# Another order for the tiles of the wide value group, and the convolution step ahead of the scans on DVE

## The reference

```python
hn = rmsnorm(x, norm_g)
z = jnp.einsum('bsd,de->bse', hn, w_in)
(aq, ak, av, ag, mq, mk, mv, mo, mi, mf, mg, gq, gk, gv, ga, gg) = jnp.split(z, split_idx, axis=-1)
att = band_chunk_attention(aq, ak, av, rel_bias)
y_a = att * jax.nn.silu(ag)
qk = jax.nn.silu(causal_conv(jnp.concatenate([mq, mk], axis=-1), conv_w))     # 4 taps
h_ml = mlstm_chunkwise(mq_c, mk_c, mv, mi + b_gates[:6], mf + b_gates[6:])
y_b = jax.nn.sigmoid(mo) * head_rmsnorm(h_ml, ml_norm_g, 6) * jax.nn.silu(mg)
log_alpha = jax.nn.log_sigmoid(jnp.einsum('bsr,rk->bsk', ga, w_alpha) + b_alpha) / 16
...
return x + jnp.einsum('bse,ed->bsd', jnp.concatenate([y_a, y_b, y_c], axis=-1), w_out)
```

## Time and profile before

| | |
|---|---|
| median of 3 runs | 1580.49 us (1580.3 to 1581.3) |
| the profiled execution | 1579.18 us, span 1577.5 us |
| instructions | 22092 |
| PE busy | 1531.3 us (97% of the span) |
| DVE, ACT, POOL busy | 826.8, 721.6, 318.2 us (52%, 46%, 20%) |
| mean granted TensorE clock | 0.992 of full speed |
| DMA | 127.99 MB, 81 GB/s on average |

### The profile page before, as it was taken

How to read it: one execution, slowest core, us unless ns; L and a number is a source line. 1 busy time by engine, 2 the same in 40 slices (tenths; PEclk the granted TensorE clock), 3 DMA queues, 4 the chain that set the end, 5 groups by cost and what they waited for, 6 DMA issues and landing times. The chain is left out here.

```text
span 1577.5 us, 22092 instructions
## 1 busy us (share of the span) xinstructions
PE 1531.3 (97%) x8990; PEld 1293.9 (82%) x8990; DVE 826.8 (52%) x1412; ACT 721.6 (46%) x1404; POOL 318.2 (20%) x273
## 2 busy tenths in 40 slices
PE   7998999999999999999999999999999999999999
PEld 6777888899889887788888888768887888888887
DVE  5326556657435754755334544568956644244442
ACT  4325554556664644544224443467854534133431
POOL 1000133101340001244103431032001343014420
PEclk9989999999999999999999999999999999999999
DMA  7212112223231102233323232110013323223331
GB/s 243 68 54 67 54 54 68 90 101 111 78 95 41 41 1 94 81 107 114 100 75 99 93 119 82 50 44 14 15 54 93 94 96 122 90 80 94 110 112 45
DMA packets 37518, 127.99 MB, mean 81 GB/s; under 512 B 4248, under 2 KB 8872, under 8 KB 37416
## 3 DMA queue, kind: packets, MB, share of 16 engines
q1 hardware_dynamic: 37416, 126.57, 25.1%
HBM read 124.46 MB, written 2.10 MB: 80 GB/s over the span
## 5 line engine op out<-in xcount | busy, mean ns | idle before, releaser
L321 PE MATMUL bank<-hhi,whi 128*128 128x512 f32 x1056 | 415.7, 394 | 4.5 <-ACT hhi L1970 1.8
L323 PE MATMUL bank<-hhi,wlo 128*128 128x512 f32 x1056 | 412.0, 390 | 0.0
L322 PE MATMUL bank<-hlo,whi 128*128 128x512 f32 x1056 | 411.7, 390 | 0.0
L312 DVE TENSOR_TENSOR wlo<-wstage,whi 128x1024 fp32r<-128x1024 f32 (+10 forms) x250 | 278.9, 1118 | 110.2 <-ACT whi L302 109.8
L302 ACT CAST whi<-wstage 128x1024 fp32r<-128x1024 f32 (+10 forms) x250 | 236.0, 948 | 136.8 <-PE bank L323 132.5
L321 PEld LDWEIGHTS bank<-hhi,whi 128*128 128x128 f32 x1056 | 198.1, 188 | 51.0 <-ACT hhi L1970 4.2
L2455 DVE SCALAR_TENSOR_TENSOR cr<-bank,vc,cr 128x511 f32<-128x511 f32 (+1 forms) x168 | 125.9, 749 | 217.1 <-ACT cr L2394 214.1
L323 PEld LDWEIGHTS bank<-hhi,wlo 128*128 128x128 f32 x1056 | 197.9, 187 | 42.3
L322 PEld LDWEIGHTS bank<-hlo,whi 128*128 128x128 f32 x1056 | 198.1, 188 | 41.3 <-issue 0.5
L2394 ACT ACTIVATE cr<-bank,vc 128x512 f32<-128x512 f32 x84 | 65.5, 780 | 248.5 <-PE bank L323 246.1
L2500 POOL TENSOR_TENSOR cr<-cr,cr 128x512 f32<-128x512 f32 x44 | 94.1, 2140 | 315.6 <-DVE cr L2455 280.9
(11 more groups left out here) (418 smaller groups left out, 2304.3 us busy)
## 6 DMA issues: line engine op xcount, KB each, us to landing
wstage<-in_wts SPq DMA_DIRECT2D x147, 512.0 KB, 3.5
wstage<-in_wts SPq DMA_DIRECT2D x32, 704.0 KB, 4.1
wstage<-in_wts SPq DMA_DIRECT2D x12, 768.0 KB, 4.6
xT<-in_x SPq DMA_DIRECT2D x4, 512.0 KB, 5.2
xt<-in_x SPq DMA_DIRECT2D x4, 512.0 KB, 5.6
out<-ob SPq DMA_DIRECT2D x8, 256.0 KB, 2.3
U<-in_rel_ext SPq DMA_DIRECT2D x6, 256.0 KB, 9.3
wstage<-in_wts SPq DMA_DIRECT2D x2, 618.0 KB, 3.8
```

The lines of the kernel that those rows point to most:

```text
L312: e.tensor_tensor(K.wlo[i % 3][:, p], K.stage[i % 3][:, p], K.whi[i % 3][:, p].bitcast(F32), SUB).then_inc(*K.dve.up(("wlo", i) if last el ...
L321: e.matmul(o, lh, rh, start=start, stop=False)
L322: e.matmul(o, lh, rl, start=False, stop=False)
L323: return e.matmul(o, ll, rh, start=False, stop=stop)
```

## The change

In `pe_den` the six products of a pair (part, tile) come in another order: the even tile goes through parts 0 and 1, then the odd tile through part 0; in the second step the even tile through part 2, then the odd one through 1 and 2. The steps keep 9 and 7 K tiles. A tile's bank is taken just before its first product, no longer both at the start. In `dve_den` the taps of block 1 and the product of block 3 come before the gate chain. Two waits of DVE for its own results are added, for `FA` behind the chain and for `amr` ahead of `sela`.

```diff
@@ -607,12 +607,13 @@
     parts = {}
-    for two in ((0, 1), (2, 3)):
-        for c in two:
-            K.RP.take(q, ("mv", 0, "c", c))
-        for n, (part, c) in enumerate((p, c) for p in range(3) for c in two):
-            if c == two[0]:
-                i, hi, lo = parts[part] = parts.get(part) or K.chunk(q, "mv", 0, part)
+    for a in (0, 2):
+        for n, (part, c) in enumerate(((0, a), (1, a), (0, a + 1), (2, a), (1, a + 1), (2, a + 1))):
+            if part == 0:
+                K.RP.take(q, ("mv", 0, "c", c))
+            if part not in parts:
+                parts[part] = K.chunk(q, "mv", 0, part)
+            i, hi, lo = parts[part]
             b = K.bank(("mv", 0, "c", c))
             for k in range(3 * part, min(8, 3 * part + 3)):
                 q.wait_ge(*K.at((x.gen, "lo", k)))
@@ -850,6 +851,8 @@
     conv(3)
     conv_silu(0)
     yield
+    conv(1)
+    conv_silu(3)
     ones6 = K.ones[32:38, 0:1].to_broadcast([6, T])
     dve_log_sigmoid(e, q, K, "fr", K.fr, 6)
     e.tensor_tensor_scan(K.Fsum, ones6, K.fr, 0.0, MUL, ADD).then_inc(*K.dve.up("Fsum"))
@@ -860,8 +863,7 @@
     ...
     e.tensor_tensor(K.em, K.Fsum, K.Am, ADD).then_inc(*K.dve.up("FA"))
-    conv(1)
-    conv_silu(3)
+    q.wait_ge(*K.at("FA"))
     yield
     conv(4)
     conv_silu(1)
@@ -869,6 +871,7 @@
     ...
     e.tensor_tensor(K.amr[32:38, :], K.Am, K.amr[0:6, :].bitcast(F32), SUB).then_inc(*K.dve.up("amr"))
+    q.wait_ge(*K.at("amr"))
     e.tensor_tensor(K.sela[:], K.ident[0:64, 0:6], K.ident[0:64, 32:38], ADD).then_inc(*K.dve.up("sela"))
```

## The result

The changed kernel takes 1569.22 us in the median of 4 runs (1566.53 to 1569.89), the kernel before 1580.39 us in 4 runs beside and ahead of them (1578.03 to 1581.3). The ratio is 0.9928 with a 95% interval of 0.9911 to 0.9946, 11.4 us less. The forecast was 1568.0 us in a range of 1564.5 to 1573.0.

What follows compares the result with a forecast made beforehand. PE bounds the kernel, with idles awaiting PSUM banks and low clock behind them. Gains of 4.3 (first pair), 2.75 (second pair) and 5.4 us (DVE's order) sum to 12.5 us, giving 1568.0 us, range 1564.5 to 1573.

Steps and rivals of the forecast that it cites:

- What bounds: Whole kernel: PE, busy 97% of the span, sets the end; its four idles between 60 and 200 us await PSUM banks.
- First pair, 4.3 us: Wide value group, first tile pair: the 2.64 us idle and 1.67 us of low clock behind it go.
- Second pair, 2.75 us: Wide value group, second tile pair: 1.13 us of idle and 1.62 us of low clock saved, 1.07 us idle stays.
- The 1.68 us: PE's idle before the first convolution group: ACT's order and copy of tile 2 are as before, nothing gained.
- DVE's order, 5.4 us: Before `mo`: tile 0's 6.92 us idle goes, tile 1 starts 7.04 us earlier after 2.1 us idle, less 1.62 us low clock.
- The rule beside the rows: Idle before tile 1 of `mo`: DVE's PSUM copy doesn't cool PE, so no clock cost; the sum would be 14.1 us.
- That what is earlier stays earlier: Behind the change: PE has no idle of half a microsecond until 238 us, and engines await no DMA, so gains stay.
- a sign of being wrong: Stages behind 200 us: if they take longer than before, the prediction is wrong.
- Nine of nine are harmless: Later in the trace, 238.54 to 1206.18 us: nine lone idles of 0.5 to 1.3 us have clock 1.00 behind them.
- The rival that the low clock comes back elsewhere: At the nine later idles: one to four get low stretches, 1.62 us each, 1569.6 to 1574.5 us; chance 0.12.
- The slower case: At the nine later idles: low stretches of 2.20 us each cost 19.8 us, giving 1587.8 us; chance 0.04.
- the failure of the pairs: Value pairs: they gain nothing because the waiting matmul has a second reason; 5.4 us left, 1575.1 us; chance 0.08.

Runs made afterwards that it cites:

- e5: Against the changed kernel, a pair takes both banks before its first product, product order kept; 1574.07 us, ratio 0.9969 to the kernel before.
- second pair of traces: The changed kernel and the kernel before, each traced once more without a change; 1568.4 us and 1581.32 us.
- e3: Against the changed kernel, DVE makes the next weight chunk's low half behind the taps of block 4; 1564.9 us, ratio 0.9903 to the kernel before.

## Why the prediction was right, step by step

*What bounds.* Right. PE, and within it a bank wait; moving only the take moves the time (e5), and the two parts add up.

*First pair, 4.3 us.* Right in both terms: the idle is gone and so is the low stretch. The cover was put at 1.0 us; `akl` ends at 75.45 and tile 1 begins behind the 18 matmuls at 76.25, 0.8 us. Whether the low stretch would have been there is less sure than the sum says, since one trace of four with the 2.64 us lacks it.

*Second pair, 2.75 us.* Right: 0.98 us of idle against 1.07, with the full clock behind.

*The 1.68 us.* Unchanged, as said. That it can be had with another place for a cast on ACT I did not see.

*DVE's order, 5.4 us.* Right in all parts. The rule beside the rows, by which the new idle would have cost no clock and the sum been 14.1 us, did not hold: the clock is low behind the 1.90 us in all five traces that have it. The taps lie in DVE's waiting time, and tile 1 waits 1.90 us against 2.1. The 0.2 us are the reaction behind the last tap, 144.87 to 144.93 and not 0.15, and small shares along the way. The added wait costs what was put for it: the chunk starts at 141.42, 0.04 us behind the end of the chain at 141.38.

*That what is earlier stays earlier.* Right as far as the waits go. The idle at 238.54 in the earlier trace rows stands at 225.59, 12.95 us earlier, of which 0.33 us come from the start of the program: 12.6 us where 12.5 were summed. At the end of the span 10.2 us are left in these two traces. Behind 200 us the changed kernel took 2.8 us longer, which the prediction had named as a sign of being wrong. It goes with low clock elsewhere, 5.1 us more by the count than in the trace of before; how the smaller figure follows from the larger was not worked out. In the second pair of traces the sign is absent: 13.0 us earlier at the same wait (225.54 against 238.51), 12.9 at the end of the span.

*The clock.* This is the term that was judged on too little. "Nine of nine are harmless" held for one execution; in others the first of them, at 220 to 239 us, has a low stretch behind it in 4 of 10 traces. The idle of 1.96 us at 1062 us was not among the rows, though it has low clock behind it before the change, and its stretch came to 5.1 us by the count in the first trace of the changed kernel, where the forecast's dearest was 2.20.

In the stretch of the change the forecast held: PE's working time at low clock fell from 7.4 to 3.4 us by the count, 4.0 where 3.9 were summed, and its idle between 60 and 200 us by 8.9 us (13.4 to 4.6), where 8 to 9 were. Outside it low clock came back in the first trace, so that PE's busy time is the same over the whole span. In the second pair it is 1534.2 and 1530.1 us, 4.1 less.

The rival that the low clock comes back elsewhere thus happened in one pair of traces and not in the other. Its reason, that things had moved, is neither shown nor excluded; that the amount also differs between runs of one kernel is shown, and the times go with it: the runs of the kernel before with a mean granted clock of 0.996 took 1574.2 and 1574.6 us, the one with 0.988 took 1586.0. That the median came within 1.2 us of the forecast is therefore in part luck; the 12.6 us at the wait behind the change are not. The slower case and the failure of the pairs did not come.

## What to carry to other kernels

Take a PSUM bank just before its first product, and begin a pair with all the work that needs only the bank that is already free; the cover is the number of those matmuls times their distance. When two pieces of work stand in one engine's list, put first the one that another engine waits for, if the second has to wait for its input anyway, and look at once for what stands between that and the next release, because the wait moves there. Judge a clock effect from several traces: count how often an idle of a certain length and place has low clock behind it, and don't take one execution for the rule.

## What the runs showed of the hardware

The same idle of PE is not always followed by the same clock. Over ten traces, the 1.2 GHz level came behind idles of 0.74 to 0.98 us in the stretch of the change in none of 10 cases, behind the one of 1.18 to 1.22 us at 220 to 239 us in 4 of 10, behind 1.68 us in 7 of 9, behind 1.90 us in 5 of 5, behind 2.20 us in 4 of 4, behind 2.64 us in 3 of 4, behind 6.92 us in 3 of 3. So it is rarer behind short idles, but length isn't all. Behind 1.95 to 1.98 us near 1050 us it came at once in 8 of 10 traces, behind 1.53 us at 294 us in the second trace of the kernel before not, and in e3 it came behind 0.93 us at 276 us. What else decides is open.

By the clock each stretch came to 1.7 us or a multiple, in time to 1.5 or 1.6 us for the shortest. So an idle that is brought from 1.9 to under 1 us can gain more than its length: 1.14 us of idle and about 1.6 us of clock in e3. The Trainium skill, "TensorE: Matmul & The Clock Gate", section "Loop structure matters more than you think", has it that a copy out of PSUM by DVE doesn't cool PE. Its loop has the next tile's matmuls follow immediately; here PE waits 1.9 us for DVE's last read of a bank, and the clock fell each time.
